# Mixer and output stage in one block; the first tile of the output projection computed inside the mixer's last step

## The reference

```python
u  = rmsnorm(x, pre_mix_gain)
p  = u @ w_in                                   # 1024 -> 3072 + 8 gate columns
y_rg = rmsnorm(rg_lru(conv4(p.rg_x)) * gelu(p.rg_gate), rg_out_gain)     # 512 features
y_ml = head_rmsnorm(sigmoid(p.o) * mlstm(silu(conv4(p.q)), silu(conv4(p.k)), p.v, p.i, p.f))   # 4 heads of 128
x  = x + rmsnorm(concat(y_rg, y_ml) @ w_out, post_mix_gain)              # 1024 -> 1024
x  = x + rmsnorm(square(relu(rmsnorm(x, pre_mlp_gain) @ w_up)) @ w_down, post_mlp_gain)        # 1024 -> 4096 -> 1024
```

## Time and profile before

| | |
|---|---|
| median of 3 runs | 2356.05 us |
| profiled execution | 2354.95 us |
| its span, first to last instruction | 2353.3 us |
| PE busy | 2295.8 us, 98% |
| DVE, ACT, POOL busy | 1083.0 us (46%), 647.1 us (27%), 767.6 us (33%) |
| mean granted PE clock | 0.987 |
| HBM | 186.53 MB read, 58.85 MB written |

### The profile page before, as it was taken

One profiled execution on the slowest core, in us unless ns is written; L12 is line 12 of the kernel. 1 busy time (PEld: TensorE's weight loads), 2 busy tenths in 40 slices (PEclk: granted clock), 3 DMA queues, 4 the chain that ended last, 5 costly groups with the idle time before them and its releaser, 6 DMA issues.

```text
span 2353.3 us, 28971 instructions
## 1 busy us (share of the span) xinstructions
PE 2295.8 (98%) x10581; PEld 1892.7 (80%) x10581; DVE 1083.0 (46%) x1651; ACT 647.1 (27%) x1185; POOL 767.6 (33%) x499
## 2 busy tenths in 40 slices
PE   8999999999995999999999999999999999999997
PEld 6777888888884888788888888888888888888886
DVE  6677657566663555433333333333633333323324
ACT  5565445454553333200100100110310110110112
POOL 6011001000001001843733733743653643653531
PEclk9999999999996999999999999999999999999999
DMA  7246445354514784311211211214521211211204
GB/s 262 108 167 211 162 150 201 125 179 148 190 56 152 235 266 152 97 40 53 71 33 39 71 36 36 71 62 152 117 62 36 71 39 35 69 45 36 62 18 71
DMA packets 136231, 246.28 MB, mean 105 GB/s; under 512 B 8160, under 2 KB 57920, under 8 KB 136160
## 3 DMA queue, kind: packets, MB, share of 16 engines
q1 hardware_dynamic: 106464, 140.15, 18.0%
q0 software_dynamic: 27392, 96.88, 14.1%
q10 hardware_dynamic: 2304, 8.39, 0.9%
HBM read 186.53 MB, written 58.85 MB: 104 GB/s over the span
## 4 chain that ended last, share of the span: by engine, by line
PE 67%; DMA 0%; DVE 0%; issue 0%; ACT 0%; POOL 0%; SPq 0%; ACTq 0%; PEldq 0%; DVEq 0%; POOLq 0%
PE o_ps L1463 22%; PE o_ps L1464 22%; PE o_ps L1465 22%; PE o_ps L1486 1%; DMA o_y_lo<-ylo_d 0%; DVE o_v_t L1695 0%; POOL out L1402 0%; DVE o_acc L1668 0%; DVE o_v_lo L1703 0%; ACT o_ps L1562 0%; DVE o_acc L1731 0%; DVE o_relu L1710 0%; ACT o_h_t L1576 0%; ACT o_relu L1613 0%; SPq L1342 0%
## 5 line engine op out<-in xcount | busy, mean ns | idle before, releaser
L1421 POOL TENSOR_TENSOR w_hi<-o_w_raw,one 128x1024 fp32r<-128x1024 f32 x96 | 183.8, 1914 | 742.7 <-PE o_ps L1465 556.0
L1463 PE MATMUL o_ps<-o_v_hi,w_hi 128*128 128x512 f32 x1024 | 399.2, 390 | 3.1 <-DVE o_relu L1710 3.1
L1464 PE MATMUL o_ps<-o_v_lo,w_hi 128*128 128x512 f32 x1024 | 399.1, 390 | 0.0
L1465 PE MATMUL o_ps<-o_v_hi,w_lo 128*128 128x512 f32 x1024 | 398.9, 390 | 0.0
L1613 ACT ACTIVATE o_relu<-o_ps 128x512 f32<-128x512 f32 x128 | 76.6, 598 | 1018.1 <-PE o_ps L1465 1018.1
L1731 DVE TENSOR_TENSOR o_acc<-o_ps,o_acc 128x512 f32<-128x512 f32 x224 | 154.7, 691 | 399.7 <-PE o_ps L1465 398.3
L465 PE MATMUL m_unit_ps<-u_hi,w_hi 128*128 128x512 f32 x768 | 308.2, 401 | 0.5 <-DVE u_lo L1087 0.3
L465 PE MATMUL m_unit_ps<-u_hi,w_lo 128*128 128x512 f32 x768 | 300.0, 391 | 0.0
L465 PE MATMUL m_unit_ps<-u_lo,w_hi 128*128 128x512 f32 x768 | 299.1, 389 | 0.0
L1423 POOL TENSOR_TENSOR w_lo<-o_w_raw,w_hi 128x1024 fp32r<-128x1024 f32 x96 | 250.1, 2605 | 7.5
L1710 DVE SCALAR_TENSOR_TENSOR o_relu<-o_ps,o_relu 128x512 f32<-128x512 f32 x128 | 88.4, 691 | 339.9 <-ACT o_relu L1613 339.9
(11 more groups left out here) (293 smaller groups left out, 3402.5 us busy)
## 6 DMA issues: line engine op xcount, KB each, us to landing
o_w_raw<-in_mlp_w_up POOLq DMA_DIRECT2D x64, 512.0 KB, 4.6
o_w_raw<-in_mlp_w_down POOLq DMA_DIRECT2D x64, 512.0 KB, 3.5
u_hi<-uhi_d SPq DMA_DIRECT2D x12, 2048.0 KB, 10.8
u_lo<-ulo_d SPq DMA_DIRECT2D x12, 2048.0 KB, 15.3
w_raw<-in_w_in POOLq DMA_DIRECT2D x24, 512.0 KB, 5.1
m_rows<-rows_d SPq DMA_DIRECT2D x16, 512.0 KB, 5.3
o_y_hi<-yhi_d SPq DMA_DIRECT2D x16, 512.0 KB, 5.4
o_y_lo<-ylo_d SPq DMA_DIRECT2D x16, 512.0 KB, 6.0
```

Source lines behind the costliest of these rows:

```text
L1421: pool.tensor_tensor(w_hi[i], w_raw[i % 2][:], one_bc, ALU.mult).then_inc(w_split[i], 1)
L1463: nc.tensor.matmul(dst, sh, mh, start=(i == 0), stop=False)
L1464: nc.tensor.matmul(dst, sh, ml, start=False, stop=False)
L1465: last = nc.tensor.matmul(dst, sl, mh, start=False, stop=(i == n - 1))
```

## The change

1. Mixer and output stage share one block: no `clear_semaphores`, no barrier between them. The output stage's semaphores are the mixer's, counted on (`Sems(..., going_on)` and the `*_base` counts). DVE and ACT wait for `mixer_done` (the last `yml_lo`), POOL for that and the last stores; SP waits for the stores.
2. Tile 0's projection, 48 matmuls in four pieces of 12 (`project_first`), stands between the slots of the last step on PE. `project(1, 0)` follows, into the banks of `tr_ps`; only its second piece waits for `mixer_done`.
3. Tiles run in the order 0 to 15. The y of tiles 0 to 7 is loaded by SP in step 15 and behind it into the buffers of u (`load_y_first`: 16 DMAs), tiles 8 and 9 after the gains. SP now loads x of tile 0 and the gains first.
4. w_out tiles 6 and 7 are loaded and split by POOL during the mixer, at the start of the last group, into tiles of their own (`w67_hi`, `w67_lo`).
5. DVE's low parts of weight tiles o and g move from the end of a group's last step into the next step, behind `weigh_queries` (`late_low_of`).
6. The gate product has 16 columns (hi and lo of w_in's 8 beside one another) and two matmuls a tile instead of three; the two halves are added by DVE after the reload (`gates_summed`).
7. In steps 0 to 3 DVE does `states` before `one_minus_a2` and `convolve("k")` after `head_numerator`; `decay_rates` goes to the end of step 0; ACT's `gate_exponential` moves between two of its `exponentials`.
8. In MLP chunk 0 the transposes of tile 15 stand before the fourth up product instead of behind it, and ACT and DVE evacuate them before their third unit (`between`).

```diff
@@ class Sems
-    def __init__(self, nc, k, prefix, names, credit):
-        self.credit = credit
+    def __init__(self, nc, k, prefix, names, credit, going_on=None):
+        self.base = STEPS if going_on else 0
+        self.credit = credit + self.base
@@ mixer, SP
+            def load_y_first(n):
+                sp.wait_ge(s["mm_g"], s.ready(STEPS - 2 + n // CPT))
+                for dst, src in (("y_first_hi", "yhi_d"), ("y_first_lo", "ylo_d")):
+                    sp.dma_start(k[dst][n].bitcast(F32), k[src][:, :, n * P:(n + 1) * P]).then_inc(k["y_first_in"][n], 16)
             load_rows(STEPS - 1)
+            sp.wait_ge(yrg_out, 32 * (STEPS - 1))
+            sp.wait_ge(yml_out, 32 * (STEPS - 1))
+            for n in range(CPT):
+                load_y_first(n)
             store(STEPS - 2)
+            for n in range(CPT, 2 * CPT):
+                load_y_first(n)
             store(STEPS - 1)
@@ mixer, POOL
                 if c < 3:
                     load_raw(c + 3, NG - 1)
+                elif c < 5:
+                    pool.dma_start(w_raw[c - 3][:].rearrange("p k f -> p (k f)"), a["w_out"][0, (c + 3) * P:(c + 4) * P, :]
+                                   ).then_inc(k["raw_in_o"][c - 3], 16)
                 else:
                     load_w_out(c - 3)
             load_gate_w(NG - 1)
+            for c in range(2):
+                pool.wait_ge(k["raw_in_o"][c], 16)
+                raw = w_raw[c][:].rearrange("p k f -> p (k f)")
+                pool.tensor_tensor(k["w67_hi"][c][:], raw, k["one"][:].broadcast_to([P, D]), ALU.mult
+                                   ).then_inc(k["w67_split"], 1)
...
+                pool.tensor_tensor(k["w67_lo"][c][:], raw, k["w67_hi"][c][:].bitcast(F32), ALU.subtract
+                                   ).then_inc(k["w67_split"], 1)
+                pool.wait_ge(k["w67_split"], 2 * c + 2)
+                load_w_out(c)
@@ mixer, PE
-                    for z, (w, x) in enumerate(((wif_hi, u_hi), (wif_hi, u_lo), (wif_lo, u_hi))):
-                        last = nc.tensor.matmul(n_ps[0:2 * NG, :], w[:, c, :], x[:, p % 2, c, :],
+                    for z, x in enumerate((u_hi, u_lo)):
+                        last = nc.tensor.matmul(n_ps[0:4 * NG, :], wif_parts[:, c, :], x[:, p % 2, c, :],
...
-            for slot in slots:
-                slot(STEPS - 1)
+            def project_first(part, h, bank, taken):
+                if taken:
+                    pe.wait_ge(s[taken], s.ready(STEPS - 1))
+                if not part and not h:
+                    pe.wait_ge(k["y_first_in"][0], 16 + 32)
+                for u in UNITS[part * 4:part * 4 + 4]:
+                    pe.wait_ge(w_split[u], NG * 2 + 2)
+                if part:
+                    pe.wait_ge(k["w67_split"], 4)
+                y_hi, y_lo = k["y_first_hi"][0], k["y_first_lo"][0]
+                cols = slice(h * 512, (h + 1) * 512)
+                for c in range(part * 4, part * 4 + 4):
+                    nc.tensor.matmul(bank, y_hi[:, c, :], w_out_hi[c][:, cols], start=(c % 4 == 0), stop=False)
+                    nc.tensor.matmul(bank, y_hi[:, c, :], w_out_lo[c][:, cols], start=False, stop=False)
+                    last = nc.tensor.matmul(bank, y_lo[:, c, :], w_out_hi[c][:, cols], start=False, stop=(c % 4 == 3))
...
+            gates_and_transposes(m, lambda: project_first(0, 0, k["ps"][:, 0, :], "xx"))
+            scores(m)
+            project_first(0, 1, k["ps"][:, 1, :], "xo")
+            state_terms(m)
+            project_first(1, 0, k["ps"][:, 2, :], "xg")
+            numerators(m)
+            project_first(1, 1, k["ps"][:, 3, :], None)
+            square_sums(m)
+            head_transposes(m)
@@ mixer, DVE
                 if mix:
                     weigh_values(m)
                     weigh_queries(m)
+                late_low_of("o")
+                late_low_of("g")
...
-                if project and not (isinstance(p, int) and p == 0):
+                if project and not gates:
                     convolve("k", p, g_p)
+                if mix and not gates:
+                    one_minus_a2(m)
                 if mix:
+                    states(m)
+                if mix and gates:
                     one_minus_a2(m)
-                    states(m)
...
+                if project and gates and p:
+                    convolve("k", p, g_p)
...
-                low_of("o")
-                low_of("g")
+                if isinstance(p, int) and p == 0:
+                    decay_rates()
@@ output stage, SP
-            load_y(0)
-            load_y(1)
+            load_x(0)
             load_gains()
-            load_x(0)
             load_x(1)
+            load_y(TB)
+            load_y(TB + 1)
@@ output stage, POOL
-            split_round(0, "out", 0)
+            pool.wait_ge(*k["mixer_done"])
+            for stored in k["y_stored"]:
+                pool.wait_ge(*stored)
@@ output stage, PE
                 for h in range(HALVES):
                     cols = slice(h * 512, (h + 1) * 512)
+                    if n == 1 and not part and h:
+                        pe.wait_ge(*k["mixer_done"])
...
                 for h in range(HALVES):
-                    if h and between:
-                        between()
...
+                        if between and n == FC - 1:
+                            between()
...
-            for n in range(NC):
+            for n in range(1, NC):
                 project(n, 0)
@@ output stage, ACT
-            with act.Fori(0, NF) as f:
+            ready("v", NC - 1)
+            chunk(0, 0, between=lambda: tile_evac(NC - 1))
+            with act.Fori(1, NF) as f:
@@ hybrid_layer
-            build_mixers(nc, a, k)
-            clear_semaphores(nc, k)
...
-            build_output(nc, a, k, out)
+        with nc.Block() as block:
+            build_mixers(nc, a, k, block)
+            mixer_consts.close()
+            build_output(nc, a, k, out, block)
```

More of the change, by code:

```diff
@@ L68, in give_credit @@
     def give_credit(self, engine, names):
+        more = self.credit - self.base - (1 if self.base else 0)
         for n in names.split():
-            engine.sem_inc(self.by_name[n], self.credit)
+            if more:
+                engine.sem_inc(self.by_name[n], more)
     def ready(self, step):
@@ L1137, in decay_rates, with period @@
                 nc.vector.tensor_scalar(k["neg_rate"][:], lam_s[:], -8.0, None, ALU.mult).then_inc(rate_made, 1)
-            def period(p, g_p, g_m, project, mix, before=None, split=False):
+            def period(p, g_p, g_m, project, mix, before=None, split=False, late=None):
                 m = p - 1
@@ L1144, in low_of, with late_low_of @@
                         split_low(u, g_p)
+                def late_low_of(u):
+                    if late is not None:
+                        split_low(u, late)
                 gates = isinstance(p, int) and p < NT
@@ L1252, in _, with build_output @@
                     p = g * NT + t
-                    period(p, g, g + (-1 if t < 1 else 0), True, True, before=g + (-1 if t < 2 else 0), split=(t == NT - 1))
-            period(STEPS, NG, NG - 1, False, True, before=(STEPS - 2) // NT)
+                    period(p, g, g + (-1 if t < 1 else 0), True, True, before=g + (-1 if t < 2 else 0), split=(t == NT - 1),
+                           late=g + -1 if t == 0 else None)
+            period(STEPS, NG, NG - 1, False, True, before=(STEPS - 2) // NT, late=NG - 1)
             head_low(STEPS - 1, NG - 1)
-def build_output(nc, a, k, out):
+        k["pe_sems"] = [s[n] for n in PE_S.split()]
+        k["act_sems"] = [s[n] for n in ACT_S.split()]
+        k["dve_sems"] = [s[n] for n in DVE_S.split()]
+        k["y_in"], k["y_in_base"] = u_out, 32 * len(U_PARTS) * 2
+        k["xh_in"], k["xh_in_base"] = u_in, 32 * (STEPS - NT) // 2
+        k["v_out"], k["v_out_base"] = [yrg_out, yml_out], 32 * (STEPS + 1)
+        k["v_back"], k["v_back_base"] = [wif_in, bias_in], [16, 32]
+        k["gains_in"], k["gains_in_base"] = par_in, 16 * 11
+        k["w_split"] = [w_split[u] for u in UNITS] + [const_made, ident_made]
+        k["w_split_base"] = [NG * 2] * 6 + [6, 0]
+        k["fin_out"] = raw_first + k["x_in"] + [k["gates_out"]]
+        k["fin_out_base"] = [32] * 3 + [32] * 4 + [16 * NT]
+        k["mixer_done"] = (s["yml_lo"], s.ready(STEPS - 1))
+        k["y_stored"] = ((yrg_out, 32 * (STEPS + 1)), (yml_out, 32 * (STEPS + 1)))
+def build_output(nc, a, k, out, block):
     NB = 2
@@ L1708, in chunk @@
                     U = (f + B * NF) * 8 + n
+                    if first and not B and n == 2:
+                        tile_evac(NC - 1)
                     dve.wait_ge(s_ff["relu"], s_ff.ready(U))
```

318 lines of the change are left out of this document (164 added, 154 removed).

## The result

The changed kernel takes 2336.11 us (median of 4, 2335.55 to 2337.04) against 2355.40 before (median of 4, 2352.41 to 2356.38): a ratio of 0.9923, 95% interval 0.9912 to 0.9935. So it is faster by 19 us (0.8%); I had said 34 (2321.2), with a range that ended at 2334. The profiled execution has a span of 2333.9 us against 2353.3, 19.4 us less.

The account below looks back on a forecast made before the run. PE was taken to bound the kernel, busy 2295.8 of 2353.3 us. The terms -12 + 3 - 20 - 4.7 = -33.7 took 2354.95 to 2321.2 us, range 2312 to 2334.

Parts of the forecast that it names:

- Steps 0 to 3: Mixer's first steps: shorter gate products, earlier PE start, half clock and numerator waits gone, 12 us saved (5 to 13).
- DVE paces: Rival: DVE's chain paces steps 0 to 3, fewer gate matmuls buy nothing: 7 us less, 2328 us; 9 in 100.
- PE waits again in steps 1 to 3: Sign that would show the forecast wrong; numerators of steps 1 to 3 were expected without a wait.
- Step 12: Mixer group change: POOL's splits of two tiles delay DVE's instructions ahead of the states, +3 us (0 to +8.6).
- The stage change: Mixer to output stage: one PE wait of 9.8 us for the gains replaces 17.6; 20 us gained (15 to 24).
- the preload of y: Rival: y loads on SP's in-order queue hold up store 15 and the mixer, slower, 2381 us; 3 in 100.
- MLP chunk 0: First MLP chunk: the 3.1 us wait and its 1.6 us of half clock go, 4.7 us saved (0 to 5).
- the last step: Mixer's last step: L484's wait gone, no PE gap over 2.5 us before tile 1, mixer's end at 734.0.
- the splits cost all: Rival: POOL's splits cost their whole 8.6 us in step 12, 2326.8 us; 9 in 100.
- the gains land late: Rival at the change of stages: the gains come at 752, 2326.7 us (5.5 later); 14 in 100.

Follow-up runs that it names:

- order_back: The changed kernel with DVE's old order in steps 1 to 3, second convolution and the recurrence's first product ahead of the states: 2337.78 us, ratio 0.9925.
- the experiment: The changed kernel with the last tile's transposes and evacuations put back to their old places in the first MLP chunk: 2340.73 us, ratio 0.9946.
- w67_later: The changed kernel with POOL's four splits of the last two W_out tiles waiting for DVE's three convolutions of step 12: 2329.96 us, ratio 0.9893.
- best_a: The changed kernel, W_out splits behind steps 12 and 13's convolutions, add freed from gains, two gains loaded first, POOL's weight loads later: 2317.32 us, ratio 0.9842.

## Why the prediction was wrong

**Steps 0 to 3 (-12, measured -4.1): the step that failed most.** The working took three gate products at 1.85 us, 5.5 us, and the numerators' waits, 2.0, as time won. That holds where PE is what the next thing waits for. Here PE waited at the numerators of these steps already before (L523 four times, of which three are there). The row calls the releaser "issue", but DVE's last state update ends 0.2 us ahead of the numerators (149.68 and 149.90 before, 143.44 and 143.65 after), and the waits follow DVE's order (order_back). So PE's shorter work only made its waits longer: with all the matmuls back the fourth numerators are 0.2 us later. Of the four gate products the last two lie between the first gate matmuls of step 1 and the fourth numerators; for them and the waits I had 5.7 us, and this stretch gives 0.1. With the short products and DVE's old order it takes 170.3, more than the 168.0 before; what makes it longer, beside the sum of the two gate halves that DVE now does, is not shown.

In step 0 I had PE go on 2.9 us earlier at the group on m_prev. It gets there at 62.22 instead of 62.80, 0.6 us earlier, and without the wait of 3.2, because it has stood 4.3 us at the bank of the v projection: POOL's splits end at 41.85 (41.07 before), the gate rows are fetched behind them, ACT's queue stands for DVE's first result from these rows (12.1 us idle until 45.17) and holds the copy of v that frees PE's bank. PE came there at 41.8, 3.8 us sooner than before, and waited 4.3. The 1.6 us of half clock and one product's 1.85 did come, which makes the 4.0 us at the first gate matmuls. The chain from POOL is read from the timelines; no run moves POOL's splits in step 0.

```profile
45.17 0.31 ACT L772 ACTIVATE m_r_z<-m_r_abs 16x128 f32<-16x128 f32 x1 [12.10 <-DVE m_r_abs L1168]
45.39 0.57 ACT L717 ACTIVATE m_v_t<-m_unit_ps 128x512 f32<-128x512 f32 x1
```

DVE's order decides how much of this lead is left at the fourth numerators: 2.4 us less with the old one in steps 1 to 3, and about 1.6 less with the decay rates put back. That DVE paces these steps was my rival with 9% and 2328 us, which leaves 5 us; with 4.1 it was the right one, and the term is below its lower end. The sign "PE waits again in steps 1 to 3" came true. Why the waits on m_prev (1.5 and 1.0) are new is not tested.

**Step 12 (+3, measured +7.6): right mechanism, one DVE instruction too few.** That POOL's splits stretch DVE's instructions with all inputs in SBUF to POOL's end, and let the updates with an input in PSUM pass, is what the rows show. The start was right, though by luck: I had 567.6 in the old frame (the times of the kernel before, here 4.1 us more), with tile 7's load; it is 563.65 + 4.1 = 567.8, right behind the gate weights' loads, for the first pair waits for tile 6 alone, and that load was issued at 537.73. What I left out is the second convolution. The late splits of o and g stand ahead of it too, so it runs until 566.34 + 2.35 = 568.7, and POOL's first instruction hits it (4.21 us for 2.55). The product then hangs on POOL's second instruction and the state copy on the third, where I had them on the first and second: the states end at 576.9 in the old frame and not at 573.7, and the numerators are 5.8 us late and not 2.5. And I left out the matmuls at 0.43 us behind a wait of this length, 1.8 us. My upper end for this term was 8.6, so it was held. The Trainium skill ("SBUF — State Buffer", section Who interferes with whom) names the two kinds that are shut out, two inputs in SBUF or a two-port mode, and counts TENSOR_SCALAR among the operations that can run in such a mode. The state copy, a TENSOR_SCALAR with one tensor in SBUF, took 2.41 us instead of 0.28; L914, whose 1891 ns I called agreement, is a TENSOR_SCALAR too. Neither has two tensors in SBUF, and no row says in which mode they ran, so the rows neither bear the rule out for them nor contradict it. An instruction with one input isn't safe by that alone.

**The stage change (-20, measured -17.8): right, the landing mis-sized.** Waits and order came as written. The mixer's last instruction is 0.2 us earlier against the frame (I had 1.1), SP passes its wait for the stores at 738.6 in the old frame (here 3.4 us less) and not at 736.7, the gains take 9.6 us and not 8, the slow matmuls cost 1.3 and not 2.7. POOL's 1 MB, which my estimate by bytes did hold, makes 2.3 us of the landing. My range for it, until 751 in the old frame, held 749.6. Store 15 was issued at 735.5 in the old frame, so the preload of y did not hold the mixer up.

**MLP chunk 0 (-4.7, measured -5.1; 5.4 by the experiment): right.** So was the loss of the waits at L484 and L532 in the last step; in its place came 2.3 us at L678 for the low part of g, which I had as one of at most 2.5.

**The range.** 2336.1 lies 2.1 us above its end. Three rivals, priced at 2326.7 to 2328, don't exclude each other: DVE paces (+6.8), the splits cost all (+5.6), the gains land late (+5.5). The end of 2334 is two of them at once (2333.6). All three came in part: 7.9 + 4.6 + 2.2 - 0.4 = 14.3 us, of the 14.9 between forecast and result. The upper end should have held three at once, 2339.1. At the lower end the sums come out differently as well: 2321.2 - 1.0 - 3.5 is 2316.7 and not 2315, and less 2.7 it is 2314.0 and not 2312.

## What to carry to other kernels

Before a shorter piece of work on an engine is counted as time won, look for the nearest wait of that engine behind it: if there is one on another engine, the gain ends there, and an experiment that makes the piece longer again shows it in one run. Work put on GpSimd is not free because GpSimd is idle: find what VectorE does at that time, and hold the work back by a semaphore until VectorE has left the critical chain; one line was worth 6.3 us here with both tiles behind one step's convolutions (w67_later), and the whole 7.6 with one tile in each of two steps (best_a). Where stages meet, check of each wait whether the instruction behind it needs what it waits for, and keep loads that are wanted late behind those that are wanted now (together 11 us here, best_a's 19 less the 7.6). And rivals that touch different places add up; the range must hold them together.
